# Hybrid decoder layer on one core: scores and values side by side on TensorE in stick-breaking and in the dilated blocks, and the second norm's sum one tile later

## Chip, cores, metric

The kernel runs on one core of one Trainium2 chip. The metric is the device time of one execution in microseconds (us), the median of the runs. A profiled execution has two figures: its own time, and its span from the first to the last instruction.

## What is computed

One decoder layer on x of 1024 positions by 1024 channels: a SwiGLU block, a mixing block with three branches that are gated and added, and a second SwiGLU block, each behind an RMSNorm. The parts around the change:

```python
h = _rmsnorm(x, mix_norm[l])
proj = h @ w_in[l]      # q, k, v of stick-breaking | q, k, v of dilated | q of memory attention | gates

# stick-breaking, 6 heads of 64, blocks of 128 queries
z = einsum('bqhd,bkhd->bhqk', qb, k) * scale
log_beta = log_sigmoid(z)
log_keep = where(causal, log_sigmoid(-z), 0.0)
after = cumsum(log_keep, axis=3, reverse=True) - log_keep
a = where(causal, exp(log_beta + after), 0.0)
o = einsum('bhqk,bkhd->bqhd', a, v)

# dilated, 3 groups of 2 heads, (w, d) = (128,1), (512,4), (2048,16)
logits = einsum('bqhd,bqkhd->bhqk', qb, kg) + bias
p = exp(logits - logsumexp(logits))
out_g = einsum('bhqk,bqkhd->bqhd', p, vg)      # the groups are combined by their softmax denominators

merged = g0 * (o_sb @ w_br_sb) + g1 * (o_dil @ w_br_dil) + g2 * (o_x @ w_br_x)
x = x + merged @ w_out
```

## The kernel before

**Data.** Everything is kept transposed, channels on partitions and positions on the free axis. A dense product (a projection, a gate, the SwiGLU blocks) is made of units: one unit is a weight tile of 1024 x 128, loaded by SyncE into `raw`, and split in two parts, `w_hi` by ScalarE (L641) and `w_lo` by VectorE (L1011). The activations are split likewise (`h_hi`, `h_lo`). For each of eight tiles k and each half of the positions TensorE runs three matmuls of 128x512: `w_hi` by `h_hi`, `w_hi` by `h_lo`, `w_lo` by `h_hi`. All dense matmuls use the full array of 128 rows by 128 columns.

**Narrow matmuls.** A head has 64 channels. So scores (`sb_scores`, `d_scores`) contract over 64 rows, two heads next to each other in the rows of the array (64*128 in the profile), and values (`sb_values`, `d_values`) give 64 columns, two heads next to each other in the columns (128*64). Below, "mode" is one of these three shapes: full, 64 rows, 64 columns.

**Order.** There is no scheduler. Each engine's program is written out by hand, and the engines wait for one another by semaphores only. On every engine an instruction that waits holds all that is written behind it.

**Second norm.** Ahead of the projections `norm_sum(1)` (L1689) adds the squares over the channels with four matmuls by a matrix of ones, from `acc_hi` and `acc_lo`, which GpSimd writes last (L570). TensorE runs `proj(PR_SB)`, then `norm_sum(1)`, then `proj(PR_SB + 1)` (L1933 to L1935). The last works on PSUM pair 1, the sum on pair 3.

**Stick-breaking** (L1955) has 36 steps, 12 for each of three pairs of heads. A step takes 128 keys against up to 512 queries; the widths in a pair are 128, 256, 384, 512, 512, 512, 512, 512, 128, 256, 384, 512. In pass s of the loop TensorE runs, in this order:
- `sb_scores(s + 2)`: six matmuls, mode 64 rows
- now and then `v_turn` (four transposes) or `xq_sum` (two matmuls)
- `beside(s, 0, 2)`: two of the four tiles of dense work that belong to the pass (six matmuls), unless `v_turn` or `xq_sum` stands there
- `sb_carry(s - 1)`: four full matmuls that add to the running sum in PSUM. It waits for `sb_added`, and reports by `sb_rest` that `sp_hi` and `sp_lo` are read
- `sb_values(s - 1)`: mode 64 columns, waits for `sb_a_ready`
- `beside(s, 2, 4)`: the other six dense matmuls
- `sb_within(s)`: four full matmuls that read `sp_hi` and `sp_lo`, and report by `sb_tri`

`sb_carry` is left out in the last step of a chain (steps 7 and 11 of a pair).

VectorE in pass s (L1357): `sb_add(s - 1)` (L1293, waits for `sb_tri`), `sb_softplus(s + 1)` (L1277, then `sp_hi` L1284, which waits for `sb_rest` of step s - 1, then `sp_lo` L1286), in every fourth pass `split_lo` (L1011), in some even passes `qk_lo` (L1320, waits for ScalarE's `qk_hi`), in odd passes `beside_copy` (L1311, L1314), which empties the one PSUM bank of the dense work. ScalarE in pass s (L878): `sb_weights(s - 1)` (L845, the exponential, waits for `sb_added`), `sb_explog(s + 2)` (Abs L831, Exp L833, Copy L835, Ln L839; Abs waits for the scores), `qk_hi` (L851), in every fourth pass `split_hi` (L641). `beside` in an even pass begins a new half and waits until `beside_copy` has emptied the bank (`bs_copied`).

**Dilated blocks** (L2076) have 32 passes n. `d_scores(n + 2)` in even n makes the scores of two blocks; it waits for `d_biased`, VectorE's L1429. `fill(n)` is six dense matmuls of a gate. `d_turn(n)` (L2041) transposes the block's probabilities, waits for ScalarE's exponential (`d_exp`, L927), and ScalarE then empties the bank (`d_evacuate`, L823). `d_values(n - 2)` in even n waits for that.

Of the kernel before, what the change touches and what calls it, by code (L numbers as in the profile page):

```python
# [121 lines left out]
PR_SB, PR_DIL = 4, 7  # L122
# [53 lines left out]
def chain_first(s):  # L176
    return s % PAIR_STEPS in (0, 8)
# [25 lines left out]
def half_done(s):  # L203

    return s // 2 if s % 2 and s >= 0 else None


def is_v(half):
    return half is not None and half // 2 % 3 == 2
# [3 lines left out]
def xq_at(s):  # L213
    return (s - 28) // 2 if s >= 28 and s % 2 == 0 else None
# [11 lines left out]
def layer(nc, x, mem, weights, gains, head_gains, rel_bias, consts, onehot, out):  # L226
    ctx = ExitStack()
    with ctx:
# [1317 lines left out]
        def _(pe):  # L1546
# [142 lines left out]
            def norm_sum(r):  # L1689

                pe.wait_ge(acc_done, 7 * r + 7)
                if r == 0:
                    pe.wait_ge(mT_done, DT)
                elif r == 1:
                    pe.wait_ge(down_added, DT * NGRP)
                else:
                    pe.wait_ge(x_added, DT)
                if r:
                    pe.wait_ge(acc_split, r)
                for c in (0, 512):  # L1700
                    if r:
                        mm(ps[:, 3, c:c + 512], ones_r[:], acc_hi[r][:, c:c + 512], True, False)
                        last = mm(ps[:, 3, c:c + 512], ones_r[:], acc_lo[:, c:c + 512], False, True)
                    else:
                        last = mm(ps[:, 3, c:c + 512], ones_r[:].bitcast(F32), acc[:, c:c + 512], True, True)
                last.then_inc(ss_done, 1)

            def proj(n, hi, lo, there=None, k0=0, k1=DT):

                kind, w = PROJ[n]  # L1710
                if k0 == 0:
                    pe.wait_ge(split_done, proj_unit(n) + 1)
                    if n < PR_DIL:

                        if n == PR_DIL - 1:
                            pe.wait_ge(newton, 4)
                        else:
                            after(pe, pr_copied, n - 1)
                    else:

                        pe.wait_ge(pr_copied, n if n == PR_DIL else n - 1)
                        after(pe, pr_kept, kept_before(n - 1))
                        if PROJ[n - 2][0] == "turn" or n == PR_DIL:
                            pe.wait_ge(pr_final, aux_before(n - 1 if n > PR_DIL else n))
                if n == PR_SB:
                    streamed(proj_pair(n), proj_unit(n) % NW, h_hi_done, h_ready, 8).then_inc(unit_done, 1)
                    return
                last = product(proj_pair(n), proj_unit(n) % NW, hi, lo, w, there=there, k0=k0, k1=k1, to=proj_from(n))
                if k1 == DT:
                    last.then_inc(unit_done, 1)  # L1730
# [150 lines left out]
            def sb_values(s):  # L1881

                p, c, j, a = sb_step(s)
                if chain_first(s):
                    after(pe, sb_o, chains_before(s))
                if s % PAIR_STEPS == 0 and p:
                    pe.wait_ge(bs_v, 2 * p)
                pe.wait_ge(sb_a_ready, s + 1)
                for h in range(2):
                    r = h * HD  # L1890
                    last = mm(sb_out_bank[r:r + HD, a:], sb_v[p % 2][:, j, r:r + HD], sb_weights_of(s)[:, h, a:], chain_first(s), j == 0)
                last.then_inc(sb_av, 1)
# [38 lines left out]
                mm(xq_bank(q), head_r[:], xq_sq_lo[:, half_of(q)[1]], False, True).then_inc(xq_sums, 1)  # L1931

            proj(PR_SB, hh, hl)  # L1933
            norm_sum(1)
            proj(PR_SB + 1, hh, hl)  # L1935
            proj(PR_SB + 2, hh, hl)

            def x_scores(n):
# [14 lines left out]
            proj_aux(PR_SB + 2)  # L1953
            beside(0, 0, 4)
            for s in range(SB_STEPS):  # L1955
                if s + 2 < SB_STEPS:
                    sb_scores(s + 2)
                if is_v(half_done(s - 1)):
                    v_turn(half_done(s - 1))
                if xq_at(s) is not None:  # L1960
                    xq_sum(xq_at(s))
                early = 0 if not s or is_v(half_done(s - 1)) or xq_at(s) is not None else 2
                if early:
                    beside(s, 0, early)
                if s:
                    sb_carry(s - 1)
                    sb_values(s - 1)
                if s:
                    beside(s, early, 4)
                else:  # L1970
                    pe.wait_ge(pr_final, aux_before(PR_DIL))
                sb_within(s)
# [103 lines left out]
            for n in range(DN):  # L2076
                if n % 2 == 0 and n + 2 < DN:
                    d_scores(n + 2)
                if n % 8:
                    fill(n)  # L2080
                d_turn(n)
                if n == 2:
                    pe.wait_ge(pr_final, aux_before(len(PROJ)))
                if n % 2 == 0 and n:
                    d_values(n - 2)
                if n % 8 == 0 and n:
                    fill(n)
            d_values(DN - 2)

# [143 lines left out]
```

## Time and profile before

| | us |
|---|---|
| median of 3 runs | 2343.32 |
| lowest, highest | 2341.65, 2344.09 |
| the profiled execution, its own time | 2342.55 |
| its span | 2340.8 |

| stretch of the span, us | what runs |
|---|---|
| 0 to 777 | first SwiGLU block, first projection of the mixing block streamed |
| 777 to 800 | second norm's sum, projections of the first pair of heads |
| 800 to 1028 | stick-breaking |
| 1028 to 1150 | memory attention and projections for the dilated blocks |
| 1150 to 1234 | dilated blocks |
| 1234 to 2341 | gates, branches, output projection, second SwiGLU block |

A timeline row gives the start in us, the duration, and in brackets how long the engine had been idle and what released it. Matmuls overlap: a full 128x512 matmul is shown with 0.39 us, and the next one starts 0.23 us after it. So the distance between starts is what a matmul costs in a row of them, and the 0.39 us is the time until its result is there.

### The profile page before, as it was taken

To read this page: it belongs to the slowest core of one execution; us is meant where nothing else is said; L and a number is where in the kernel's file an instruction comes from. 1 tells how busy PE (TensorE), PEld (TensorE's weight loads), DVE (VectorE), ACT (ScalarE), POOL (GpSimd) and SP (SyncE) were. 2 spreads that over 40 slices of the span, in tenths; PEclk is the share of its full clock that TensorE was granted. 3 is DMA by queue.
4 is the path that set the end of the run, shared out by engine and by line. 5 is a ranking of instruction groups with operands and counts; after the bars stand their busy time and mean duration, and the time that the engine had idled before them with its cause. 6 is when DMAs were issued, how large, how long until landed. Compare 5 with 4: busy or idle time off the path is not lost.

```text
span 2340.8 us, 25824 instructions
## 1 busy us (share of the span) xinstructions
PE 2312.7 (99%) x10616; PEld 1859.5 (79%) x10616; DVE 1148.9 (49%) x1119; ACT 620.4 (27%) x800; POOL 137.6 (6%) x108
## 2 busy tenths in 40 slices
PE   8999999999999999999999999999999999999998
PEld 7888888888887766667778888888888888888887
DVE  8443444443445677777636343445344434444434
ACT  6211111111112567756443111223111111111111
POOL 3000000000001321212000000011000000000000
PEclk9999999999999999999999999999999999999999
DMA  5211111111112200001122111131111111111112
GB/s 161 76 45 54 45 49 40 54 45 54 45 54 61 108 28 19 19 28 55 37 28 64 54 54 45 55 117 53 47 52 48 45 54 45 48 42 54 45 54 72
DMA packets 47424, 125.78 MB, mean 54 GB/s; under 512 B 4285, under 2 KB 20829, under 8 KB 47104
## 3 DMA queue, kind: packets, MB, share of 16 engines
q1 hardware_dynamic: 45456, 112.61, 15.9%
q10 hardware_dynamic: 912, 10.11, 1.1%
q0 software_dynamic: 992, 2.15, 0.5%
q8 instruction: 48, 0.79, 0.1%
q14 instruction: 16, 0.13, 0.0%
HBM read 116.42 MB, written 9.87 MB: 54 GB/s over the span
## 4 chain that ended last, share of the span: by engine, by line
PE 93%; DVE 5%; ACT 1%; issue 1%; POOL 0%; DMA 0%; SPq 0%; DVEq 0%; ACTq 0%
PE ps L1548 91%; DVE h_lo L1018 1%; DVE w_lo L1011 0%; DVE sb_a L1293 0%; PE ps L2041 0%; DVE xT L1082 0%; DVE xT L1194 0%; DVE h_lo L1474 0%; PE ps L1984 0%; PE ps L2135 0%; DMA raw<-in_weights 0%; ACT sb_a L845 0%; ACT sb_l L833 0%; ACT sb_l L831 0%; PE ps L1757 0%
## 5 line engine op out<-in xcount | busy, mean ns | idle before, releaser
L1548 PE MATMUL ps<-h_hi,w_hi 128*128 128x512 f32 x2240 | 876.7, 396 | 2.7 <-ACT w_hi L641 2.3
L1548 PE MATMUL ps<-h_lo,w_hi 128*128 128x512 f32 x2240 | 862.6, 390 | 0.8 <-DVE h_lo L1474 0.4
L1548 PE MATMUL ps<-h_hi,w_lo 128*128 128x512 f32 x2240 | 699.9, 390 | 0.0
L1548 PEld LDWEIGHTS ps<-h_hi,w_hi 128*128 128x128 f32 x2240 | 420.2, 188 | 128.0 <-issue 40.5
L1548 PEld LDWEIGHTS ps<-h_hi,w_lo 128*128 128x128 f32 x2240 | 420.8, 188 | 88.9
L1548 PEld LDWEIGHTS ps<-h_lo,w_hi 128*128 128x128 f32 x2240 | 420.3, 188 | 85.8 <-DVE h_lo L1474 1.7
L641 ACT ACTIVATE w_hi<-raw 128x1024 fp32r<-128x1024 f32 x196 | 204.2, 1051 | 791.5 <-PE ps L1548 771.0
L1011 DVE TENSOR_TENSOR w_lo<-raw,w_hi 128x1024 fp32r<-128x1024 f32 x196 | 249.7, 1282 | 159.1 <-ACT w_hi L641 150.2
L1082 DVE TENSOR_TENSOR xT<-xT,ps 128x1024 f32<-128x1024 f32 x175 | 213.3, 1219 | 181.2 <-PE ps L1548 181.2
L1548 PE MATMUL ps<-a_hi,w_hi 128*128 128x512 f32 x704 | 276.8, 393 | 5.6 <-DVE w_lo L1011 4.9
L1548 PE MATMUL ps<-a_lo,w_hi 128*128 128x512 f32 x704 | 275.1, 391 | 0.0
L1548 PE MATMUL ps<-a_hi,w_lo 128*128 128x512 f32 x704 | 218.1, 391 | 0.0
L1048 DVE SCALAR_TENSOR_TENSOR glu<-ps,rB 128x1024 f32<-128x1024 f32 x44 | 53.9, 1224 | 265.1 <-PE ps L1548 265.1
L1041 DVE TENSOR_TENSOR silu<-ps,rB 128x1024 f32<-128x1024 f32 x44 | 53.8, 1224 | 252.1 <-PE ps L1548 252.1
L677 ACT ACTIVATE silu<-silu 128x1024 f32<-128x1024 f32 x44 | 46.6, 1060 | 439.6 <-DVE silu L1041 439.6
L1548 PEld LDWEIGHTS ps<-a_hi,w_hi 128*128 128x128 f32 x704 | 133.1, 189 | 35.3 <-DVE w_lo L1011 5.7
L1548 PEld LDWEIGHTS ps<-a_hi,w_lo 128*128 128x128 f32 x704 | 132.7, 189 | 27.8
L1548 PEld LDWEIGHTS ps<-a_lo,w_hi 128*128 128x128 f32 x704 | 133.0, 189 | 27.1
L567 POOL TENSOR_TENSOR acc<-acc,sq 128x1024 f32<-128x1024 f32 x21 | 51.9, 2470 | 1090.5 <-ACT sq L648 1090.5
L1414 DVE TENSOR_TENSOR gate<-ps,rB 128x1024 f32<-128x1024 f32 x24 | 29.4, 1224 | 128.2 <-PE ps L1548 128.2
L941 ACT ACTIVATE gate<-gate 128x1024 f32<-128x1024 f32 x24 | 25.0, 1058 | 172.7 <-DVE gate L1414 172.5
L1066 DVE TENSOR_TENSOR glu<-glu,silu 128x1024 f32<-128x1024 f32 x44 | 53.9, 1224 | 4.4
(224 smaller groups left out, 1589.4 us busy)
## 6 DMA issues: line engine op xcount, KB each, us to landing
raw<-in_weights SPq DMA_DIRECT2D x196, 512.0 KB, 3.5
x_keep<-xT ACTq DMA_DIRECT2D x1, 4096.0 KB, 12.3
x_back<-x_keep ACTq DMA_DIRECT2D x1, 4096.0 KB, 13.4
x_nat<-in_x SPq DMA_DIRECT2D x7, 512.0 KB, 7.4
out<-y_nat SPq DMA_DIRECT2D x7, 512.0 KB, 3.2
toe_keep<-toe_row ACTq DMA_DIRECT2D x2, 704.0 KB, 6.1
m_nat<-in_mem SPq DMA_DIRECT2D x1, 1024.0 KB, 8.4
d_fB<-d_f_keep POOLq DMA_DIRECT2D x2, 512.0 KB, 6.5
```

What stands on the lines that cost most here:

```text
L567: nc.gpsimd.tensor_tensor(acc[:], acc[:], sq[:, k % 2, :], ALU.add).then_inc(acc_done, 1)
L641: nc.scalar.activation(w_hi[:, k % NW].rearrange("p a b -> p (a b)"), raw[:, k % NRAW, :], ACT.Copy).then_inc(hi_done, 1)
L677: nc.scalar.activation(silu[:, t % 2, :], silu[:, t % 2, :], ACT.Silu).then_inc(silu_done, 1)
L941: nc.scalar.activation(gate_tile(m, b), gate_tile(m, b), ACT.Sigmoid).then_inc(gate_done, 1)
L1011: nc.vector.tensor_tensor(w_lo[:, k % NW].rearrange("p a b -> p (a b)"), raw[:, k % NRAW, :], w_hi[:, k % NW].rearrange("p a b -> p (a b)" ...
L1018: nc.vector.scalar_tensor_tensor(out=h_lo[:, k, :], in0=xT[:, k, :], scalar=g32[:, gain, k:k + 1], in1=h_hi[:, k, :].bitcast(F32), op0=ALU ...
L1041: nc.vector.tensor_tensor(silu[:, t % 2, :], ps[:, 0, :], rB[:], ALU.mult).then_inc(gate_scaled, 1)
L1048: nc.vector.scalar_tensor_tensor(out=glu[:, t % 2, :], in0=ps[:, 1, :], scalar=0.5, in1=rB[:], op0=ALU.mult, op1=ALU.mult).then_inc(up_sca ...
L1066: nc.vector.tensor_tensor(glu[:, t % 2, :], glu[:, t % 2, :], silu[:, t % 2, :], ALU.mult).then_inc(glu_done, 1)
L1082: nc.vector.tensor_tensor(xT[:, m, :], xT[:, m, :], ps[:, 2 + m % 2, :], ALU.add).then_inc(down_added, 1)
L1414: nc.vector.tensor_tensor(gate_tile(m, b), ps[:, merge_pair(m, b), :], rB[:], ALU.mult).then_inc(mg_taken, 1)
L1548: return pe.matmul(o, a, b, start=start, stop=stop, skip_group_check=True)
```

## The change

Three edits, all in TensorE's program. No instruction is added or taken away, and the other engines' programs are the same.

```diff
             proj(PR_SB, hh, hl)
+            proj(PR_SB + 1, hh, hl, k1=1)
             norm_sum(1)
-            proj(PR_SB + 1, hh, hl)
+            proj(PR_SB + 1, hh, hl, k0=1)
             proj(PR_SB + 2, hh, hl)
...
             for s in range(SB_STEPS):
+                early = 0 if not s or is_v(half_done(s - 1)) or xq_at(s) is not None else 2
+                if early:
+                    beside(s, 0, early)
                 if s + 2 < SB_STEPS:
                     sb_scores(s + 2)
                 if is_v(half_done(s - 1)):
                     v_turn(half_done(s - 1))
                 if xq_at(s) is not None:
                     xq_sum(xq_at(s))
-                early = 0 if not s or is_v(half_done(s - 1)) or xq_at(s) is not None else 2
+                if s and not early:
+                    sb_carry(s - 1)
+                if s:
+                    sb_values(s - 1)
                 if early:
-                    beside(s, 0, early)
-                if s:
                     sb_carry(s - 1)
-                    sb_values(s - 1)
                 if s:
                     beside(s, early, 4)
                 else:
...
             for n in range(DN):
                 if n % 2 == 0 and n + 2 < DN:
                     d_scores(n + 2)
-                if n % 8:
-                    fill(n)
-                d_turn(n)
                 if n == 2:
                     pe.wait_ge(pr_final, aux_before(len(PROJ)))
                 if n % 2 == 0 and n:
                     d_values(n - 2)
-                if n % 8 == 0 and n:
+                d_turn(n)
+                if n:
                     fill(n)
             d_values(DN - 2)
```

TensorE's order in pass 4 of stick-breaking, before (`sb_qk` are the scores, `h_` the dense work, `sp_` the carry, `sb_a` the values):

```order
L1548 MATMUL ps<-sb_qk 128x512 x6
L1548 MATMUL ps<-h_hi,w_hi 128x512
L1548 MATMUL ps<-h_lo,w_hi 128x512
L1548 MATMUL ps<-h_hi,w_lo 128x512
L1548 MATMUL ps<-h_hi,w_hi 128x512
L1548 MATMUL ps<-h_lo,w_hi 128x512
L1548 MATMUL ps<-h_hi,w_lo 128x512
L1548 MATMUL ps<-sp_hi,tri 128x512 x2
L1548 MATMUL ps<-sp_lo,tri 128x512 x2
L1548 MATMUL ps<-sb_a_104,sb_v_99 64x512 x2
```

The same pass, changed:

```order
L1548 MATMUL ps<-h_hi,w_hi 128x512
L1548 MATMUL ps<-h_lo,w_hi 128x512
L1548 MATMUL ps<-h_hi,w_lo 128x512
L1548 MATMUL ps<-h_hi,w_hi 128x512
L1548 MATMUL ps<-h_lo,w_hi 128x512
L1548 MATMUL ps<-h_hi,w_lo 128x512
L1548 MATMUL ps<-sb_qk 128x512 x6
L1548 MATMUL ps<-sb_a_104,sb_v_99 64x512 x2
L1548 MATMUL ps<-sp_hi,tri 128x512 x2
L1548 MATMUL ps<-sp_lo,tri 128x512 x2
```

The dense tiles now stand ahead of the scores, the values directly behind them, and the carry behind the values. In both orders the pass goes on with six dense matmuls and `sb_within`. Passes with `v_turn` or `xq_sum` (10, 12, 22, 24, 28, 30, 32, 34) keep their order.

TensorE's order in two passes of the dilated blocks, n even and the next, before (`d_qk` are the scores, `cst,d_p` the transposes, `d_pT` the values):

```order
L1548 MATMUL ps<-d_qk 128x128 x2
L1548 MATMUL ps<-d_qk 128x256 x2
L1548 MATMUL ps<-h_hi,w_hi 128x512
L1548 MATMUL ps<-h_lo,w_hi 128x512
L1548 MATMUL ps<-h_hi,w_hi 128x512
L1548 MATMUL ps<-h_lo,w_hi 128x512
L1548 MATMUL ps<-h_hi,w_lo 128x512 x2
L2041 MATMUL ps<-cst,d_p 128x128 x2
L1548 MATMUL ps<-d_pT,d_v_113 64x128 x4
```

The same place, changed:

```order
L1548 MATMUL ps<-d_qk 128x128 x2
L1548 MATMUL ps<-d_qk 128x256 x2
L1548 MATMUL ps<-d_pT,d_v_113 64x128 x4
L2045 MATMUL ps<-cst,d_p 128x128 x2
L1548 MATMUL ps<-h_hi,w_hi 128x512
L1548 MATMUL ps<-h_lo,w_hi 128x512
L1548 MATMUL ps<-h_hi,w_hi 128x512
L1548 MATMUL ps<-h_lo,w_hi 128x512
L1548 MATMUL ps<-h_hi,w_lo 128x512 x2
```

The values move from behind the transposes to right behind the scores, and the dense matmuls from ahead of the transposes to behind them.

## Rows read from the trace of the kernel before

**Rows 1.** The page, part 4: the chain that ended last, by engine.
```profile
PE 93%; DVE 5%; ACT 1%; issue 1%; POOL 0%; DMA 0%; SPq 0%; DVEq 0%; ACTq 0%
```

**Rows 2.** Busy time by stretch: length, then each engine's us (instructions), granted TensorE clock, DMA.
```profile
736.00:747.00 11.00, 8.55 (x31) 6.72 (x30) 4.45 (x4) 5.39 (x5) 0.00 (x0) 0.84 0.64 179
...
800.00:1028.00 228.00, 221.72 (x1095) 149.43 (x1096) 172.29 (x203) 164.22 (x216) 50.86 (x52) 1.00 0.07 21
...
1150.00:1234.40 84.40, 82.84 (x531) 59.51 (x530) 30.04 (x80) 35.59 (x101) 4.34 (x5) 1.00 0.20 26
```

**Rows 3.** Timeline of TensorE and VectorE at the last down projection and the second norm's sum.
```profile
738.77 0.79 PE L1548 MATMUL ps<-a_hi,w_hi 128*128 128x512 f32 x1 [2.45 <-DVE w_lo L1011]
...
774.78 0.73 PE L1548 MATMUL ps<-h_lo,w_hi 128*128 128x512 f32 x2 [0.27 <-DVE h_lo L1018]
777.09 0.47 PE L1548 MATMUL ps<-acc_hi,ones_r 128*128 128x512 f32 x1 [1.57 <-POOL acc_lo L570]
...
770.96 2.57 DVE L1011 TENSOR_TENSOR w_lo<-raw,w_hi 128x1024 fp32r<-128x1024 f32 x1 [0.79 <-ACT w_hi L641]
```

**Rows 4.** Timeline of TensorE in pass 5 of stick-breaking, 512 wide.
```profile
831.39 0.97 PE L1548 MATMUL ps<-sb_qk 64*128 64x512 f32 x6
832.29 0.50 PE L1548 MATMUL ps<-h_hi,w_hi 128*128 128x512 f32 x1
832.62 0.40 PE L1548 MATMUL ps<-h_lo,w_hi 128*128 128x512 f32 x1
...
834.24 0.62 PE L1548 MATMUL ps<-sp_lo,tri 128*128 128x512 f32 x2
834.79 1.08 PE L1548 MATMUL ps<-sb_a,sb_v 128*64 128x512 f32 x4
835.80 0.50 PE L1548 MATMUL ps<-h_hi,w_hi 128*128 128x512 f32 x1
```

**Rows 5.** Timeline of VectorE, passes 2 to 8 of stick-breaking.
```profile
812.52 0.68 DVE L1293 TENSOR_TENSOR sb_a<-sb_a,ps 128x512 f32<-128x512 f32 x1
...
823.28 1.22 DVE L1011 TENSOR_TENSOR w_lo<-raw,w_hi 128x1024 fp32r<-128x1024 f32 x1
824.42 0.68 DVE L1311 SCALAR_TENSOR_TENSOR pr_x<-ps,rB 128x512 f32<-128x512 f32 x1
...
831.73 0.69 DVE L1320 TENSOR_TENSOR sb_qk<-pr_x,sb_qk 128x512 fp32r<-128x512 f32 x1 [1.72 <-ACT sb_qk L851]
832.34 1.21 DVE L1293 TENSOR_TENSOR sb_a<-sb_a,ps 128x1024 f32<-128x1024 f32 x1
...
834.97 0.69 DVE L1284 CAST sp_hi<-sb_l 128x1024 fp32r<-128x1024 f32 x1 [0.28 <-PE ps L1548]
835.70 1.23 DVE L1286 TENSOR_TENSOR sp_lo<-sb_l,sp_hi 128x1024 fp32r<-128x1024 f32 x1
...
851.50 1.22 DVE L1293 TENSOR_TENSOR sb_a<-sb_a,ps 128x1024 f32<-128x1024 f32 x1 [0.24 <-PE ps L1548]
```

**Rows 6.** Timeline of ScalarE, first and last instruction of one pass.
```profile
827.23 1.00 ACT L831 ACTIVATE sb_l<-ps 128x1024 f32<-128x1024 f32 x1
...
831.08 0.62 ACT L851 ACTIVATE sb_qk<-pr_x 128x512 fp32r<-128x512 f32 x1
```

**Rows 7.** Timeline of three engines in pass 24, where the values wait.
```profile
949.35 1.22 DVE L1293 TENSOR_TENSOR sb_a<-sb_a,ps 128x1024 f32<-128x1024 f32 x1 [0.21 <-PE ps L1548]
...
950.60 1.06 ACT L845 ACTIVATE sb_a<-sb_a 128x1024 f32<-128x1024 f32 x1 [2.62 <-DVE sb_a L1293]
...
951.71 1.08 PE L1548 MATMUL ps<-sb_a,sb_v 128*64 128x512 f32 x4 [1.10 <-ACT sb_a L845]
```

**Rows 8.** Timeline of TensorE in the dilated blocks: passes 2 and 31.
```profile
1156.58 0.70 PE L1548 MATMUL ps<-d_qk 64*128 64x256 f32 x4 [0.75 <-DVE d_st L1429]
...
1232.56 0.49 PE L2041 MATMUL ps<-cst,d_p 128*128 128x128 f32 x3
1233.63 0.88 PE L1548 MATMUL ps<-d_pT,d_v 128*64 128x128 f32 x12 [0.58 <-ACT d_pT L823]
```

## Prediction

> **What bounds the kernel now.** I read the chain that ended last first: 93% of it is TensorE's [rows 1]. So what TensorE saves is saved at the end, and every wait put on it is paid in full, unless it takes the place of another. Then the stretches that the change touches: stick-breaking (228 us, TensorE busy 221.7, VectorE 172, ScalarE 164) and the dilated blocks (84.4 us, TensorE 82.8, VectorE 30, ScalarE 36) [rows 2]. The reader is to see the difference: in the dilated blocks the other engines are idle two thirds of the time, in stick-breaking VectorE and ScalarE are busy three quarters of it. A reorder costs little in the first and may cost much in the second. There I read the timelines for what a step of one engine waits for on the next.
>
> **Price of a change of mode.** In pass 5 the last part of the carry starts at 834.24; two matmuls at 0.23 end their turn at 834.70, and the values start at 834.79: 0.09 to leave a mode. The first dense matmul behind the scores stands 0.33 ahead of the next, where 0.23 is usual: 0.10 to enter the full mode [rows 4]. A switch costs about 0.2 us. (Entering the 64-column mode is nearer 0.05.)
>
> **The norm's sum.** TensorE sits idle for 1.57 us until 777.09, for GpSimd's `acc_lo` [rows 3]. Six dense matmuls of 0.227 now stand in that gap, 1.36 us. Their weights are ready: the split of that unit ended at 773.53 [rows 3]. The sum starts when it did, so the norm's chain on ScalarE and VectorE is not later, and all behind it on TensorE is 1.4 earlier. Gain 1.4.
>
> **Dilated blocks.** Before, a pair of passes goes full, 64 rows, full, 64 columns, full: four switches. Changed, it goes full, 64 rows, 64 columns, full: three. There are 14 such pairs (n = 2 to 28): 14 x 0.2 = 2.8. Does a wait come in? A pair of passes takes some 5.5 us, and ScalarE and VectorE work for under half of it. The transposes now come up to 1.4 sooner behind the scores, but they use scores made two passes earlier. Only `d_turn(1)`, now right behind `d_turn(0)`, has to wait (some 0.3), and that is hidden, since the scores in pass 2 wait 0.75 for VectorE anyway [rows 8]. At the end `d_values(30)` waited for ScalarE behind the last transposes: they start at 1232.56, three at 0.11 end at 1232.89 and leaving the mode takes 0.09, yet the values start at 1233.63, 0.65 late [rows 8]. The last `fill` now covers this. Gain 2.8 + 0.6 = 3.4.
>
> No row shows 64 rows directly followed by 64 columns. The bounds are from no cost at all (0.15 less each) to a drain on each side (0.2 more); I take the price of the other switches. For the 14 pairs this is -2.1 to +2.8. The Trainium skill's page TensorEngine Tiling (Key Properties) says that a change of tiling mode, not only of tile, drains TensorE. By it the two narrow shapes count as two modes, the saving is one switch in four and not two, and the sum stays as it stands; no run here shows it yet.
>
> **Stick-breaking, what TensorE saves.** The passes 1 to 33 less seven with `v_turn` or `xq_sum` have scores and early dense tiles: 26 passes, each one switch fewer, 26 x 0.2 = 5.2 if TensorE stays the bound. A full pass would take 6.7 instead of 6.9.
>
> **Stick-breaking, what the new order waits for.** Before, the carry waits only for `sb_add`, and frees `sp_hi` for VectorE early; the exponential on ScalarE is off this loop. Changed, the carry stands behind the values, and the values wait for the exponential. So one loop runs through all three engines. Its length at full width, from one `sb_add` to the next:
> - `sb_add` to exponential 1.25 (949.35 to 950.60), exponential to values 1.11 (to 951.71) [rows 7]
> - values to the carry 1.01 (834.79 to 835.80), the carry 0.33 + 2 x 0.23 + 0.39 until its result = 1.18 [rows 4]
> - end of the carry (834.24 + 0.62 = 834.86) to `sp_hi` 0.11 [rows 4, 5], `sp_hi` to `sp_lo` 0.73, `sp_lo` 1.14 as for `split_lo`, an operation of the same size (823.28 to 824.42) [rows 5]
> - what else VectorE has in the pass, `beside_copy` or `qk_lo`, 0.61 (831.73 to 832.34) [rows 5]
>
> The sum is 7.14, above TensorE's own 6.7. Where `split_lo` is in the pass, 1.14 more: 8.3. Before, the same loop was without 1.25, of which only the part up to the carry counted, and without 1.11 and 1.01, some 5, and TensorE's work covered it.
>
> A second loop comes from the dense tiles. In an even pass they wait for `beside_copy`, which stands behind `sp_lo`; before, the scores (0.90) stood ahead of them and gave cover. The scores now come behind them, and ScalarE's four functions behind the scores. From one `sb_add` (which directly follows `beside_copy`): 0.12 until the copy is seen, 1.39 dense, 0.09 leaving the mode, 0.97 scores [rows 4], 0.05, then Abs to `qk_hi` 3.85 (827.23 to 831.08), `qk_hi` to `qk_lo` 0.65 [rows 5, 6], and 0.61 to the next `sb_add`: 7.7.
>
> Now the first pair of heads, from `sb_add` of step 1 to that of step 7. Before it takes 851.50 - 812.52 = 39.0 [rows 5]. Changed: turn 1 to 2 by the second loop 7.7; 2 to 3 by the first with `split_lo`, 8.3 less 0.9 for the 384 wide operations, 7.4; 3 to 4 by the second 7.7; 4 to 5 and 5 to 6 by the first 7.15 each; 6 to 7 with `split_lo` 8.3, less 1.2 since the next step's `sp_hi` and `sp_lo` are 128 wide, 7.1. Sum 44.2, so 5.2 more. The first turn adds 0.3. In the narrower steps behind it (128 to 384) VectorE's and ScalarE's parts of the loop shrink and TensorE's dense work does not; there small waits and the saved 0.2 cancel: 0, between -0.8 and +1. The second pair is the same. In the third pair the even passes have no `qk_lo`, but three have `xq_sum` and keep their order: I take +4, from 2 to 5. Together 5.4 + 5.4 + 4 = 15, the 5.2 saved being inside it, since where the loop decides the switches are hidden in the wait.
>
> **The sum.** 15 - 1.4 - 3.4 = +10.2. From the profiled execution's own 2342.55 this gives 2352.8; the median of the runs lies 0.8 above that execution, so **2353.5**. Nothing behind the stretches gives time back, as TensorE goes on as the bound.
>
> **Rivals.**
> 1. The values are ready when TensorE comes, and the dense tiles find their bank empty. Then 5.2 + 1.4 + 3.4 = 10 is saved: 2333.3. For it: in all of stick-breaking TensorE waits little now (222 of 228 us busy) [rows 2]. Against it: in pass 5 the exponential follows `sb_add` (832.34) by 1.25 + 1.11, so the values could start at 834.70, and started at 834.79 [rows 4, 5, 7]: 0.1 of slack, where the new order brings them 1.0 forward. It decides from a loop under 6.7 on. I give it 7%.
> 2. The loops bind, but only in the passes with `split_lo`: about 1.7 in each of three pairs, and the other 23 passes save 4.6. Stick-breaking is then within 1 us of before up to +5, and the whole lies between 2339 and 2344. For it: VectorE might do its copies while it waits for the carry. Against: they stand behind `sp_lo` in its order and cannot. 10%.
> 3. The direct step from scores to values costs 0.2 more. In stick-breaking it mostly vanishes in the wait, in the dilated blocks it is 2.8: 2356.5. 12%.
> 4. The clock falls. In the stretch from 736 to 747 the granted clock is 0.84 on the mean, that is 3.5 us at the level of 1.2 GHz, and TensorE had been idle for 2.45 us until 738.77; half of it, 1.8 us, is what it costs [rows 2, 3]. At 777.09, after 1.57 us idle, stick-breaking ran on at 1.00 [rows 2, 3]. The longest new wait is that of the dense tiles behind `beside_copy` with `split_lo`: copy 0.68 + `split_lo` 1.14 + `sp_lo` and `sp_hi` 1.9 + 0.27 behind the carry, less TensorE's 2.3 of dense work and `sb_within`, 1.7 us, five times. If each brings a fall: + 9, 2362. 5%. The page TensorE: Matmul & The Clock Gate of the Trainium skill (HAM oscillation) warns of idle gaps between bursts of matmuls for this reason; by it the granted clock is the first thing to look at in the new trace.
>
> **Chances and range.** The forecast with the bounds of its own terms (stick-breaking +10 to +18, dilated -1 to -5) is 2348 to 2358, 66%. The range that leaves out no more than 2 in 10 reaches to rival 3 and toward rival 2: 2346.5 to 2361. About 0.2% (4.7 us) is what a measurement of this kernel can tell from no change. Faster by more than that: rival 1 and a little of rival 2, 0.08. Within it: the rest of rival 2 and the low end of the forecast, 0.11. Slower: 0.81.
>
> **What would show it.** Right: in full passes of stick-breaking `sb_add` follows `sb_add` by 7.1 to 7.8 instead of 6.1 to 7.3; the values wait for ScalarE's exponential and dense matmuls for `beside_copy` in most passes, some 26 us of TensorE's waits in the stretch (6 of before, 15, and the 5.2 of the switches); the stretch is about 243 us long instead of 228. The gap ahead of the norm's sum is 0.2 instead of 1.57. A pair of full passes in the dilated blocks takes 5.3 instead of 5.5, and the last values don't wait. Wrong: if the values start right behind the scores without a wait, the loop is not what I think; if the stretch is shorter than 228, rival 1 holds; if the granted clock in it is under 1.00, rival 4.

## The result

| | median of runs, us | lowest, highest |
|---|---|---|
| before | 2343.12 | 2341.65, 2344.09 |
| changed | 2357.81 | 2356.45, 2358.87 |

The changed kernel is slower: the ratio is 1.0066, 95% interval 1.0056 to 1.0076. That is 14.7 us more; 10.2 were forecast, and the time lies in the range. The profiled execution has a span of 2356.2, 15.4 more than before.

The chain that ended last, by engine, in the changed kernel (answers to [rows 1]):

```profile
PE 88%; DVE 6%; ACT 3%; issue 1%; POOL 1%; DMA 0%; SPq 0%; DVEq 0%; ACTq 0%
```

TensorE's part fell from 93% to 88%, and ScalarE's and VectorE's rose from 6% to 9%. The stretches say where. Each row has its window, its length, then busy time and instructions of TensorE's matmuls, its weight loads, VectorE, ScalarE and GpSimd, the granted clock and DMA (answers to [rows 2]):

```profile
736.00:747.00 11.00, 8.55 (x38) 6.78 (x37) 5.83 (x5) 6.39 (x6) 0.00 (x0) 1.00 0.62 181
797.00:1048.00 251.00, 222.79 (x1094) 150.14 (x1094) 167.32 (x203) 165.08 (x216) 44.74 (x52) 0.99 0.07 21
1170.20:1251.40 81.20, 79.86 (x532) 57.60 (x531) 28.97 (x77) 36.11 (x101) 4.33 (x5) 1.00 0.22 27
```

In stick-breaking TensorE does the same work in the same busy time (222.8, before 221.7), and the stretch is 251 us long instead of 228. The dilated blocks are 3 shorter. The granted clock in the first row is 1.00, where it was 0.84.

Measured exactly, from the first scores to the first matmul of memory attention, and so on, the difference of the two spans is made of this:

| part | difference, us |
|---|---|
| up to the second norm's sum | -1.35 |
| its sum and the projections behind it | -1.35 |
| stick-breaking | +22.9 |
| memory attention, projections | 0.0 |
| dilated blocks | -3.3 |
| all behind | -1.5 |

The first and the last row lie where nothing was edited; they are two falls of the clock that the profiled execution of before had and this one has not. The first is the 0.84 above; the second shows as 0.89 over the 16 us from 2300 in the kernel before, where the changed one has 1.00 at the same place (from 2315.4).

The norm's sum, timeline of TensorE in the changed kernel (answers to [rows 3]; in brackets the idle time ahead and what ended it):

```profile
775.74 0.47 PE L1548 MATMUL ps<-acc_hi,ones_r 128*128 128x512 f32 x1 [0.20 <-POOL acc_lo L570]
```

The gap is 0.20 instead of 1.57.

The dilated blocks, timeline of TensorE in the changed kernel (answers to [rows 8]): two rounds of scores and values, and a wait.

```profile
1214.03 0.93 PE L1548 MATMUL ps<-d_qk 64*128 64x128 f32 x8
1214.89 0.88 PE L1548 MATMUL ps<-d_pT,d_v 128*64 128x128 f32 x12
...
1219.28 0.93 PE L1548 MATMUL ps<-d_qk 64*128 64x128 f32 x8
...
1225.18 0.93 PE L1548 MATMUL ps<-d_qk 64*128 64x128 f32 x8 [0.59 <-DVE d_st L1429]
```

and the same place before:

```profile
1201.13 0.93 PE L1548 MATMUL ps<-d_qk 64*128 64x128 f32 x8
1201.99 0.50 PE L1548 MATMUL ps<-h_hi,w_hi 128*128 128x512 f32 x1
...
1206.63 0.93 PE L1548 MATMUL ps<-d_qk 64*128 64x128 f32 x8
```

A pair of passes takes 5.25 (1214.03 to 1219.28) instead of 5.50. The scores are followed by the values after 0.86, and before they were followed by dense work after 0.86 too: the direct step from 64 rows to 64 columns costs what a step to the full mode costs. The last values, at 1250.57, no longer wait.

Stick-breaking, timeline of three engines over one turn of the changed kernel, from step 5 to 6 (answers to [rows 4 to 7]; a turn is the way from one `sb_add` to the next):

```profile
840.56 1.21 DVE L1293 TENSOR_TENSOR sb_a<-sb_a,ps 128x1024 f32<-128x1024 f32 x1
...
841.80 1.06 ACT L845 ACTIVATE sb_a<-sb_a 128x1024 f32<-128x1024 f32 x1 [2.23 <-DVE sb_a L1293]
...
842.92 1.08 PE L1548 MATMUL ps<-sb_a,sb_v 128*64 128x512 f32 x4
...
843.92 0.74 PE L1548 MATMUL ps<-sp_hi,tri 128*128 128x512 f32 x2
...
845.23 0.69 DVE L1284 CAST sp_hi<-sb_l 128x1024 fp32r<-128x1024 f32 x1 [2.32 <-PE ps L1548]
...
845.96 1.23 DVE L1286 TENSOR_TENSOR sp_lo<-sb_l,sp_hi 128x1024 fp32r<-128x1024 f32 x1
...
847.10 0.69 DVE L1320 TENSOR_TENSOR sb_qk<-pr_x,sb_qk 128x512 fp32r<-128x512 f32 x1
...
847.70 1.22 DVE L1293 TENSOR_TENSOR sb_a<-sb_a,ps 128x1024 f32<-128x1024 f32 x1
```

It can be followed as one loop: add 840.56, exponential 841.80, values 842.92, carry 843.92, `sp_hi` 845.23, `sp_lo` 845.96, `qk_lo` 847.10, add 847.70. The steps are 1.24, 1.12, 1.00, 1.31, 0.73, 1.14 and 0.60, together 7.14. No engine is idle for want of work; each waits for the next one in the circle. `sp_hi` waits 2.32 us in this turn, where [rows 5] has 0.28.

The prediction's second loop, which begins with the dense tiles behind `beside_copy`, is the turn from step 3 to 4:

```profile
825.48 1.21 DVE L1293 TENSOR_TENSOR sb_a<-sb_a,ps 128x1024 f32<-128x1024 f32 x1
...
825.71 0.47 PE L1548 MATMUL ps<-h_hi,w_hi 128*128 128x512 f32 x1 [1.63 <-DVE pr_x L1311]
...
827.26 0.96 PE L1548 MATMUL ps<-sb_qk 64*128 64x512 f32 x6
...
828.27 1.02 ACT L831 ACTIVATE sb_l<-ps 128x1024 f32<-128x1024 f32 x1 [0.49 <-PE ps L1548]
...
832.14 0.62 ACT L851 ACTIVATE sb_qk<-pr_x 128x512 fp32r<-128x512 f32 x1
...
832.79 0.69 DVE L1320 TENSOR_TENSOR sb_qk<-pr_x,sb_qk 128x512 fp32r<-128x512 f32 x1 [0.38 <-ACT sb_qk L851]
...
833.40 1.21 DVE L1293 TENSOR_TENSOR sb_a<-sb_a,ps 128x1024 f32<-128x1024 f32 x1
```

From `sb_add` to the first dense matmul 0.23, to the scores 1.55, to Abs 1.01, to `qk_hi` 3.87, to `qk_lo` 0.65, to the next `sb_add` 0.61: 7.92.

The groups of waits in stick-breaking, changed kernel, from 798 to 1042 us: total us, times, longest.

```profile
DVE sp_hi L1284 <- PE ps L1548: 51.8, 24, 4.9
...
PE ps L1548 <- ACT sb_a L845: 18.2, 18, 2.4
...
PE ps L1548 <- DVE pr_x L1311: 4.1, 4, 1.6
...
PE ps L1548 <- DVE pr_x L1314: 2.1, 4, 0.6
```

and before, the first two of them, from 800 to 1028:

```profile
DVE sp_hi L1284 <- PE ps L1548: 19.3, 20, 1.7
...
PE ps L1548 <- ACT sb_a L845: 4.0, 6, 1.1
```

### The profile page after: what moved, and what is told of

It reads as the page before. It is cut to its first block, busy times and chain, and to the rows that moved or that the text cites. A ratio compares the mean times of both kernels' runs of the same rounds, so it can differ in the third digit from the quotient of the medians.

```text
span 2356.2 us, 25824 instructions
## 1 busy us (share of the span) xinstructions
PE 2307.2 (98%) x10616; PEld 1856.4 (79%) x10616; DVE 1144.1 (49%) x1119; ACT 622.1 (26%) x800; POOL 131.5 (6%) x108
## 4 chain that ended last, share of the span: by engine, by line
PE 88%; DVE 6%; ACT 3%; issue 1%; POOL 1%; DMA 0%; SPq 0%; DVEq 0%; ACTq 0%
PE ps L1548 87%; DVE h_lo L1018 1%; DVE sb_a L1293 1%; ACT sb_a L845 1%; DVE w_lo L1011 1%; DVE sp_lo L1286 1%; ACT sb_l L833 1%; ACT sb_l L831 1%; PE ps L2045 0%; DVE sp_hi L1284 0%; ACT sb_l L839 0%; DVE xT L1082 0%; DVE xT L1194 0%; POOL sb_l L580 0%; DVE h_lo L1474 0%
## 5 line engine op out<-in xcount | busy, mean ns | idle before, releaser
L1548 PEld LDWEIGHTS ps<-h_hi,w_hi 128*128 128x128 f32 x2240 | 420.6, 188 | 110.6 <-issue 13.6
L567 POOL TENSOR_TENSOR acc<-acc,sq 128x1024 f32<-128x1024 f32 x21 | 51.8, 2468 | 1089.5 <-ACT sq L648 1089.5
```

The source lines that it names most:

```text
L567: nc.gpsimd.tensor_tensor(acc[:], acc[:], sq[:, k % 2, :], ALU.add).then_inc(acc_done, 1)
L1548: return pe.matmul(o, a, b, start=start, stop=stop, skip_group_check=True)
```

## The experiments

In all runs the kernel before ran beside the others, and all differences are medians against it, with the ratio and its 95% interval. Where a sentence speaks of a turn, it is the distance from one `sb_add` to the next in the profile; between the kernel before and the three runs that keep its order in stick-breaking, every turn agrees within 0.07 us.

### Each edit alone, and the two that gain together

The norm edit alone:

```diff
+            proj(PR_SB + 1, hh, hl, k1=1)
             norm_sum(1)
-            proj(PR_SB + 1, hh, hl)
+            proj(PR_SB + 1, hh, hl, k0=1)
```

> The kernel before with the norm edit alone (six dense matmuls of the next projection ahead of the sum). My theory: the gap of 1.57 us ahead of the sum shrinks to 0.2, the sum starts when it did, the whole is 1.4 us shorter. Rival: the norm's chain on ScalarE and VectorE gets later with the projection work in front of it, and nothing is gained: 0, the gap reappears behind the sum or at the first scores.

Measured: 2340.00 against 2342.21, 2.2 less (0.9989, 0.9980 to 0.9998). In the trace the sum starts after a gap of 0.20, and the first scores follow it by 21.5 instead of 22.9 us: 1.34 gained. The rest of the 2.2 is inside the interval.

The dilated edit alone is the third part of the diff.

> The kernel before with the dilated edit alone. My theory: one switch of 0.2 us fewer in 14 pairs and no wait of the last values: 3.4 us shorter, a pair of full passes 5.3 instead of 5.5. Rival: the direct step from 64 rows to 64 columns costs 0.2 more, then 0.6 shorter; rival: the saving in the changed kernel came only together with the other edits, then less than 2.

Measured: 2338.05, 4.2 less (0.9983, 0.9974 to 0.9992). In the trace the blocks, from the first scores to the first matmul behind the last values, take 80.4 instead of 84.4: 4.0 gained, of it 0.97 at the last values and 0.24 in most pairs. The changed kernel gained 3.3 there, because one of its scores waited 0.59 for VectorE (the row at 1225.18), which this run doesn't show.

Both:

> Both edits, stick-breaking in the order of before. If the edits are independent: 4.7 us shorter than before (0.998), faster than both kernels. Rival: one of them lives on the other (or on where in time a fall of the clock comes): 3 us or less.

Measured: 2335.00, 7.2 less (0.9971, 0.9960 to 0.9982). It is faster than before, and some 22 us faster than the changed kernel. In its trace stick-breaking is as long as before (227.4) and the blocks take 80.4. Expected were 4.7; the two gains in the traces make 5.3, and the interval (4 to 9 us) holds both. So the 7.2 of the medians may be more than the edits alone are worth.

The stick-breaking edit alone is the second part of the diff.

> The stick-breaking edit alone. By the forecast of the prediction 15 us longer than before; by what the changed kernel measured (14.7 longer in all, with 4.7 gained elsewhere) 19 to 20 longer, and the stretch from the first scores to the memory attention 23 us longer only if the fall of the clock in the third pair is there again; without that fall 19 us.

Measured: 2363.01, 20.8 more (1.0088, 1.0074 to 1.0101). So the three edits add up: 20.8 - 7.2 = 13.6, measured 14.7.

### Which order makes the loop: two halves of the edit

Only the carry moved behind the values:

```diff
                 if early:
                     beside(s, 0, early)
-                if s:
+                if s and not early:
                     sb_carry(s - 1)
+                if s:
                     sb_values(s - 1)
+                if early:
+                    sb_carry(s - 1)
```

> The kernel before, with only one thing of the stick-breaking edit: the carry stands behind the values. The dense tiles stay between scores and values, so no switch is saved and the dense tiles keep the cover of the scores. My theory of two loops: loop 1 (add, exponential, values, carry, sp_hi, sp_lo) alone makes this 9 to 12 us longer than before, and the values wait for the exponential in many full passes. Rival A (the dense tiles behind beside_copy make all of the loss): 0 to 2 us longer. Rival B (loop 1 makes all of it): 19 or more.

Measured: 2358.17 against 2341.39, 16.8 more (1.0073, 1.0056 to 1.0090).

Only the early dense tiles moved ahead of the scores:

```diff
+                if early:
+                    beside(s, 0, early)
                 if s + 2 < SB_STEPS:
                     sb_scores(s + 2)
...
-                if early:
-                    beside(s, 0, early)
                 if s:
                     sb_carry(s - 1)
                     sb_values(s - 1)
```

> The kernel before, with only the other thing: the early dense tiles stand ahead of the scores. The carry stays ahead of the values and leaves the dense work and scores in one piece, the number of switches is one smaller only in that scores are followed by the carry. My theory: loop 2 alone (beside_copy to dense tiles to scores to ScalarE) costs 3 to 6 us, with dense matmuls waiting for beside_copy. Rival A (loop 2 makes all of the loss): 19 or more. Rival B (it costs nothing): -1 to +1.

Measured: 2347.64, 6.3 more (1.0026, 1.0016 to 1.0036).

The medians lie between the rivals in both, the first above my bound, the second just outside it. Together they are 23.1, more than the 20.8 of both at once. The turns are clearer. Timeline of VectorE's `sb_add`, steps 2 and 3 of the first pair, with the carry behind the values:

```profile
819.74 0.95 DVE L1293 TENSOR_TENSOR sb_a<-sb_a,ps 128x768 f32<-128x768 f32 x1
...
827.11 1.21 DVE L1293 TENSOR_TENSOR sb_a<-sb_a,ps 128x1024 f32<-128x1024 f32 x1
```

and with the dense tiles ahead, steps 3 and 4:

```profile
825.13 1.21 DVE L1293 TENSOR_TENSOR sb_a<-sb_a,ps 128x1024 f32<-128x1024 f32 x1
...
833.18 1.22 DVE L1293 TENSOR_TENSOR sb_a<-sb_a,ps 128x1024 f32<-128x1024 f32 x1
```

All turns of the wide steps:

| turn | before | carry behind | dense ahead | changed |
|---|---|---|---|---|
| 1 to 2 | 6.78 | 6.77 | 7.85 | 7.88 |
| 2 to 3 | 5.72 | 7.37 | 5.73 | 7.37 |
| 3 to 4 | 7.32 | 7.32 | 8.05 | 7.92 |
| 4 to 5 | 6.06 | 7.15 | 6.29 | 7.16 |
| 5 to 6 | 6.48 | 7.15 | 6.72 | 7.14 |
| 6 to 7 | 6.62 | 7.24 | 6.45 | 7.23 |

Each half brings back its own turns of the changed kernel, and leaves the others within 0.25 us of before. The turns into steps 3, 5, 6 and 7 belong to the first loop (carry behind values), those into 2 and 4 to the second (dense tiles ahead of the scores). These are the turns to which the prediction gave the one loop and the other.

### One link of the loop shortened

The stick-breaking edit alone, with a shorter exponential. It leaves out the exponential of all but 128 columns a head:

```diff
-                a = sb_weights_of(s)[:, :, sb_step(s)[3]:]
+                a = sb_weights_of(s)[:, :, sb_step(s)[3]:sb_step(s)[3] + P]
```

> The stick-breaking edit alone, with the exponential of the weights made over the first 128 columns of each head instead of up to 512; the rest is left out. That takes 0.6 us out of loop 1 in the full passes (an instruction of 0.4 instead of 1.06) and 0.6 of ScalarE's time. If loop 1 decides in the wide passes, the loss against before falls from 20.8 to 10 to 14. Rival (the values wait for something else than the exponential, or loop 2 takes over at once): it falls by less than 4.

Measured: 2355.60, 14.2 more than before, 6.6 less than with the whole exponential (1.0061, 1.0044 to 1.0077), just outside the 10 to 14 that were expected. Timeline of one turn:

```profile
849.43 1.22 DVE L1293 TENSOR_TENSOR sb_a<-sb_a,ps 128x1024 f32<-128x1024 f32 x1
...
850.68 0.42 ACT L845 ACTIVATE sb_a<-sb_a 128x256 f32<-128x256 f32 x1 [2.29 <-DVE sb_a L1293]
...
851.15 1.08 PE L1548 MATMUL ps<-sb_a,sb_v 128*64 128x512 f32 x4
...
856.12 1.21 DVE L1293 TENSOR_TENSOR sb_a<-sb_a,ps 128x1024 f32<-128x1024 f32 x1
```

The values follow the exponential by 0.47 instead of 1.12, and the turn shown, from step 6 to 7, is 6.69 instead of 7.23. The one ahead of it is 6.98 instead of 7.14, though its exponential is 0.64 shorter as well: in it the values stand directly behind the scores, and these behind dense tiles that waited 0.45 for `beside_copy`. There the next wait took over, and this is why less went away than was taken out. The turns of the second loop are unchanged (7.87, 7.94). So the exponential is a link of the first loop and not of the second.

### The wide and the narrow passes

```diff
+                new = early and 2 <= s % 12 <= 7
-                if early:
+                if new:
                     beside(s, 0, early)
```

and so on: the new order in passes 2 to 7 of each pair of heads only.

> The stick-breaking edit only in the passes 2 to 7 of each pair of heads (the wide ones), the order of before in the others. By the prediction, which put the narrow passes at nothing, this is as long as with the edit in all passes: 19 to 21 us longer than before. If the narrow passes really cost what the trace of the changed kernel seems to show (1.65 us in the first pair), some 4 to 5 us of the loss go away: 15 to 17 longer.

Measured: 2357.60, 16.2 more (1.0072, 1.0055 to 1.0089), so 4.6 less than with the edit everywhere. The complement, the new order outside these passes (`not 2 <= s % 12 <= 7`):

> The complement of the run with the wide passes: the stick-breaking edit only outside the passes 2 to 7 of each pair of heads, the order of before in the wide ones. The prediction put these passes at 0 (-0.8 to +1 a pair). If the new order costs there by its own loop of add, exponential, values and carry, as the turns into steps 9 and 11 of the changed kernel say (0.5 and 0.6 longer), this is 3.5 to 5.5 us longer than before, and together with the run of the wide passes (16.2) it makes the 20.8 of the edit in all passes. If they were late only because the wide passes ahead of them were, it is within 1 us of before.

Measured: 2346.26 against 2341.88, 4.4 more (1.0016, 1.0007 to 1.0025). 16.2 + 4.4 = 20.6, against 20.8 for the edit everywhere. This run also holds the turn from step 0 to 1 (5.50 instead of 5.09), which the prediction had. The rest is a cost of the narrow passes themselves. The profile shows which: here is the turn from step 10 (384 wide) to step 11 in the changed kernel.

```profile
873.14 0.96 DVE L1293 TENSOR_TENSOR sb_a<-sb_a,ps 128x768 f32<-128x768 f32 x1 [0.65 <-PE ps L1548]
...
874.13 0.84 ACT L845 ACTIVATE sb_a<-sb_a 128x768 f32<-128x768 f32 x1 [2.41 <-DVE sb_a L1293]
...
875.03 0.87 PE L1548 MATMUL ps<-sb_a,sb_v 128*64 128x384 f32 x4
...
876.90 0.42 DVE L1284 CAST sp_hi<-sb_l 128x256 fp32r<-128x256 f32 x1 [2.46 <-PE ps L1548]
...
877.35 0.85 DVE L1286 TENSOR_TENSOR sp_lo<-sb_l,sp_hi 128x256 fp32r<-128x256 f32 x1
...
878.13 1.21 DVE L1011 TENSOR_TENSOR w_lo<-raw,w_hi 128x1024 fp32r<-128x1024 f32 x1
...
879.26 0.68 DVE L1314 TENSOR_TENSOR pr_x<-ps,rB 128x512 f32<-128x512 f32 x1
...
879.86 1.21 DVE L1293 TENSOR_TENSOR sb_a<-sb_a,ps 128x1024 f32<-128x1024 f32 x1
```

It is the first loop again, 6.72 long where the turn was 6.12 before. The widths shrink its own parts, but `split_lo` (1.13) and `beside_copy` (0.60) are full size in it. Both were in this turn before as well; what is new is the wait, 2.46 of `sp_hi` for the carry, where it waited 1.61 before.

### The carry ahead of the scores

```diff
                 if early:
                     beside(s, 0, early)
+                    sb_carry(s - 1)
                 if s + 2 < SB_STEPS:
                     sb_scores(s + 2)
```

with the values behind the scores and no carry behind them.

> The stick-breaking edit with one thing turned back: the carry stands ahead of the scores, so that the early dense tiles, carry, scores and values follow each other. Scores and values are still next to each other, with one switch fewer. My theory: loop 1 is cut (the carry doesn't wait for the exponential), loop 2 stays and the scores come later by the carry: 8 to 13 us longer than before instead of 20.8. Rival (what costs is that scores and values stand next to each other, since the values come too soon for the exponential whatever the carry does): 18 or more.

Measured: 2357.30 against 2342.08, 15.2 more (1.0061, 1.0045 to 1.0076). Neither theory: it lies between. The waits of the stretch in this kernel name another loop:

```profile
ACT sb_l L831 <- PE ps L1548: 30.9, 24, 6.2
DVE sb_qk L1320 <- ACT sb_qk L851: 22.8, 8, 3.4
...
PE ps L1548 <- DVE sb_a L1293: 11.7, 10, 1.9
...
DVE sp_hi L1284 <- PE ps L1548: 7.4, 14, 1.0
```

`sp_hi` hardly waits (7.4, changed kernel 51.8), so the first loop is cut as I thought. But the carry now comes with only 1.4 us of dense work between it and `sb_within`, waits for `sb_add`, and holds the scores; ScalarE waits for them 30.9 us; its functions hold `qk_lo`, and `qk_lo` stands ahead of the next `sb_add`. I had left this third loop out, and no run takes it apart. In this kernel's trace the granted clock also fell several times in the stretch, which is 0.97 on the mean; the profiled execution, 2361.4, is the slowest of its four:

```profile
800.00:1046.00 246.00, 226.80 (x1079) 150.75 (x1076) 168.72 (x202) 165.96 (x216) 44.87 (x52) 0.97 0.06 19
```

### The clock in pass 31

The changed kernel with the order of before in pass 31 alone (`new = early and s != 31`).

> The changed kernel with the order of before in one pass only, 31, where TensorE was idle for 2.4 us and the granted clock then fell to the level of 1.2 GHz for 6.8 us. That turn of sb_add took 9.75 in the changed kernel, 8.47 in the run of the stick-breaking edit alone (a fall of 3.4 us) and 6.0 before. If the idle time brings the fall: no fall in this stretch, the turn is 6.0 to 6.5, and the whole 2.5 to 3.8 us shorter than the changed kernel, about 11 to 12 longer than before. If the fall comes from elsewhere (the other long waits, the weeks of full work), it is there again and the gain is under 2.

Around pass 31 of the changed kernel, timeline of GpSimd, VectorE and TensorE:

```profile
1010.41 1.63 POOL L589 TENSOR_TENSOR xq_sq_lo<-pr_x,xq_sq_hi 128x512 fp32r<-128x512 f32 x1 [1.94 <-ACT xq_sq_hi L859]
...
1010.91 2.20 DVE L1286 TENSOR_TENSOR sp_lo<-sb_l,sp_hi 128x1024 fp32r<-128x1024 f32 x1
...
1015.39 1.98 PE L1548 MATMUL ps<-sb_a,sb_v 128*64 128x512 f32 x4 [2.41 <-ACT sb_a L845]
```

and the same `sp_lo` before:

```profile
995.64 2.19 DVE L1286 TENSOR_TENSOR sp_lo<-sb_l,sp_hi 128x1024 fp32r<-128x1024 f32 x1
```

The `sb_add` behind it comes late in both kernels, 9.29 after the one ahead: VectorE has five more instructions in that turn (L1336 to L1350, for memory attention), and `sp_lo` takes 2.20 where it takes 1.23 elsewhere. Before, TensorE waited 1.03 for that `sb_add`, and the carry then filled the time of the exponential. Here the values stand first, so TensorE is idle for 2.41. The four matmuls of the values then take 1.98 instead of 1.08. The granted clock over 20 us there, changed kernel, and the kernel with the old order in pass 31:

```profile
1006.00:1026.00 20.00, 16.57 (x63) 9.96 (x62) 14.05 (x17) 10.74 (x19) 4.56 (x5) 0.83 0.08 26
```
```profile
1004.00:1024.00 20.00, 17.52 (x81) 10.54 (x79) 17.73 (x22) 12.41 (x19) 5.31 (x5) 1.00 0.09 27
```

0.83 over 20 us is 6.8 us at the level of 1.2 GHz; the kernel with the stick-breaking edit alone has 0.91 over the 20 us from 1010, which is 3.6. With the old order in this one pass the longest idle time there is 1.07, there is no fall, the turn is 6.03 (changed kernel 9.74), and stick-breaking is 246.6 long instead of 250.3. So in the trace the fall goes with the idle time, as expected. Not all of the 3.7 us is the fall, though: the kernel with only the carry behind the values was idle for 2.13 us at this place, had no fall, and its turn is 7.22, where 5.99 was before. By that some 1.2 us are the wait itself and 2.5 the fall (an estimate from these three traces). In the median it can hardly be seen: 2356.61 against 2342.08, 14.5 more (1.0060, 1.0045 to 1.0076), where the changed kernel had 14.7. I expected 11 to 12, which the interval (10.5 to 17.8) holds; whether the fall came in all executions of the changed kernel or only in the profiled one stays open.

### A tuned order

The norm and the dilated edit, and in 13 of the 26 passes another order, most often dense tiles, carry, scores, values (the other passes keep the order of before):

```diff
+            SB_ORDER = {5: 'Z3CV1', 6: '2CZV2', 7: '3CZV1', 11: '2CZV2', 13: '2ZVC2', 18: '2CZV2', 19: '3CZV1', 23: '2CZV2', 25: '2ZVC2', 27: '2CZV2', 29: '2CZV2', 31: '3CZV1', 33: '2ZVC2'}
```

Z are the scores, C the carry, V the values, digits the number of dense tiles.

> The norm and the dilated edit, and in stick-breaking the order of before except in 13 passes, where a relay of the waits by hand (durations from the trace of before) gave another order: in most of them dense tiles, carry, scores, values, so that scores and values stand next to each other with the carry ahead of both, never behind. By the relay stick-breaking is 2.6 us shorter than before, so 9 to 10 shorter than before in all (7 of the two other edits). Rival: the relay undersizes waits, as it did for the changed kernel (15 where the trace shows 21 to 23), and stick-breaking gets 1 to 4 longer: 3 to 6 shorter in all.

Measured: 2336.12 against 2342.08, 6.0 less (0.9973, 0.9962 to 0.9984). Expected were 9 to 10 less, so the relay missed: stick-breaking is 227.0 long in the trace, 0.4 shorter than before and not 2.6. This kernel is no better than the two gaining edits with the old order (0.9971), and that one is simpler.

## Why the prediction was right, and where its size was off

**Direction and mechanism: right.** TensorE was the bound, and stick-breaking had no room for a loop of three engines. The term decides the sign, and both loops were there in the turns that the prediction named.

**Price of a switch, 0.2: right.** The pair of passes went from 5.50 to 5.25, with one switch fewer. The unknown, the direct step from 64 rows to 64 columns, costs no more than the others, so rival 3 fell. The Trainium skill's page TensorEngine Tiling (Key Properties), by which every change of mode drains TensorE, agrees with that: 0.86 us from scores to what follows in either order. The runs show the price, not the drain itself.

**Norm's sum, 1.4: right** (1.35 in the trace, the gap 0.20 as forecast).

**Dilated blocks, 3.4: right** (3.3 in the changed kernel, 4.0 with the edit alone).

**Stick-breaking, +15: mis-sized.** The trace has +22.9. By parts (the prediction's own 5.2 and 0.3 make 5.5 for a pair, not 5.4; its total of 15 holds):

| part | forecast | trace |
|---|---|---|
| pair 1, `sb_add` of step 0 to that of 7 | +5.4 | +6.1 |
| pair 1, narrow steps behind | 0 | +1.65 |
| pair 2 | +5.4 | +7.15 |
| pair 3 | +4 | +8.0 |

- The first loop was 7.14 in the forecast and is 7.14 in the trace; with `split_lo` 7.1 and 7.23. The second was 7.7 and is 7.88 and 7.92: the dense tiles start 0.23 behind `sb_add` instead of 0.12, and the scores 1.55 behind these instead of 1.48.
- The step that failed first is "in the narrower steps small waits and the saved 0.2 cancel: 0". I didn't add up the loop there. With `split_lo` and `beside_copy` in it, it is 6.72 against 6.12, 1.65 a pair together. Over two pairs this is 3.2 of the missing 8.
- The second is the third pair, taken as +4, where the trace has +8.0. Of it 3.75 is the one turn around pass 31 (5.99 before, 9.74 here), some 1.2 the wait for the exponential and 2.5 the fall of the clock behind it. Rival 4 had the mechanism (a long wait brings a fall), but in the five passes with `split_lo` behind `beside_copy`, where the longest wait was 1.6 and no fall came. It came in a wait for the exponential that I hadn't listed. The other turns of the pair together have +4.2.
- The rest, 0.9 over two pairs, is mostly the second loop, whose turns are 0.2 longer than worked out.

**Waits, "some 26 us of TensorE's": nearly right in sum.** TensorE was idle for 28.2 of the 251 us (251.00 less 222.79): 18.2 for the exponential, 6.2 for `beside_copy`, the rest in smaller waits. "In most passes" said too much: in 35 passes the values waited 18 times, the dense matmuls 8 times.

**The total was nearer than its largest term** (+10.2 forecast, +14.7 by the medians, +15.4 by the spans) partly by luck: 2.9 of the missing 8 were given back by two falls of the clock that the profiled execution of before had, up to the norm's sum and at the end. The medians of the runs with one part each show the same with other numbers: 20.8 where 15 was forecast, and 7.2 given back where 4.8 was. Both were taken too small, with opposite signs.

**Rival 1 and rival 2 fell**: no turn from step 1 to step 7 of the first two pairs is under 7.14, where the forecast had 6.7 for TensorE's own work, and the passes without `split_lo` lose as well (1.10 and 0.66 in the turns into steps 5 and 6).

## What to carry to other kernels

When an order on the engine that is the bound is changed to save a fixed price (here 0.2 us a switch), walk the circle of waits through the other engines first: an instruction that frees a buffer for another engine should not stand behind one that waits for that engine's latest result. Moving it can open another circle, as the kernel with the carry ahead of the scores did, so the new order is to be walked through as well. Add up the circle for every width and every occasional extra (a weight split, a copy out of PSUM), not for the widest pass alone; extras don't shrink with the tile, and narrow passes can be bound by them. And take such an edit apart: here two of the three were worth 7.2 us by the medians (5.3 by the traces), and the third cost 20.8.

## What the runs showed of the hardware

**A fall of the clock is a matter of idle time, but not of it alone.** TensorE is idle for 2.45 us at the same place in every one of these kernels ([rows 3], 738.77 in the kernel before), and the granted clock fell there in ten of fourteen traces. It was 0.84 over these 11 us before and 1.00 in the changed kernel, with the same idle time. The 1.57 us idle ahead of the norm's sum were followed by a fall in two of nine traces that have the gap, and a shorter gap of 0.2 in none of five. The kernel with the dilated edit alone, whose first stretch is the kernel before's own, had such a fall, with 0.83 over the 10 us from 774.

Around pass 31, with the idle time ahead of the carry or the values: 2.41 (two traces), 2.32, 1.85 and 1.83 were followed by a fall, 2.13 was not, and neither were the eight from 0.99 to 1.32. Waits of 1.4 to 1.65 earlier in stick-breaking were followed by none in the changed kernel.

From the 2.45 us of idle time to the norm's sum the way is 38.32 with the fall (738.77 to 777.09) and 36.77 without (738.97 to 775.74, changed kernel), so this fall cost 1.55; the prediction had 1.8 from the clock alone. In the kernel with the dilated edit the way from the sum to the first scores is 24.5 instead of 22.9, 1.6 more. Two executions of one program can differ by that much. A profile is one draw: a difference of a fall or two between two profiles is not the edit's.

**VectorE slows beside GpSimd, in these rows where GpSimd began first.** `sp_lo` of 128x1024 takes 1.23 alone. Where GpSimd's subtraction had begun 0.5 us ahead of it, it took 2.20 (1010.91 above), and 2.19 or 2.20 at this place in 13 of the 14 traces. (In the other, with the shortened exponential, GpSimd began beside `sp_hi`, which took 1.80 instead of 0.69.) The 256 wide one in the turn from step 10 to 11 took 0.85 with GpSimd at work, and 0.83 in the same turn before (871.88). At 848.36 before it began 0.06 ahead of GpSimd and took its 0.43. So these slow instructions are in both kernels and are not what the edit costs. I had taken the durations of undisturbed instructions for the loop, and for the wide turn shown above this was right to 0.01.
